# A hybrid SSD, short-convolution and PEER layer: the dt product placed among the first convolution tiles, and x and B made token-major by VectorE block transposes

## The reference, cut to what matters

```
h      = modulate(rmsnorm(x), shift, scale)        # 512 latent tokens; the same for 256 context tokens
z, xbc, dt, ... = split(h @ w_in)                  # xbc: 2048 columns (x 1024, B 512, C 512), dt: 32 columns
xbc    = silu(dwconv5(xbc) + bias)                 # 5 taps along the tokens
dt     = softplus(dt + dt_bias);  a = -exp(a_log) * dt
acs    = cumsum(a) within chunks of 128 tokens     # then exp(acs), exp(total), exp(total - acs)
states = B^T @ (exp(total - acs) * dt * x)         # per chunk; forward and backward, then a scan over chunks
mod_l  = silu(c) @ w_ada + b_ada                   # six rows of 1024; four of them are needed late
```

## Time and profile before

| what | value |
|---|---|
| plain executions | 1876.95 us median of 3 (1876.34 to 1878.25) |
| profiled execution | 1875.16 us, of which the span is 1873.4 us and 1.8 us lie around it |
| PE busy | 1432.9 us (76%), 4441 products |
| DVE busy | 1457.8 us (78%), 2813 instructions |
| ACT busy | 546.8 us (29%) |
| POOL busy | 870.1 us (46%) |
| busy tenths of PE, first ten of 40 slices (46.8 us each) | 7 9 9 9 9 9 9 8 8 8 |
| the same of DVE | 1 5 5 6 3 6 9 7 7 3 |

### The profile page before, as it was taken

One profiled execution on the slowest core, in us unless ns is written; L12 is line 12 of the kernel. 1 busy time (PEld: TensorE's weight loads), 2 busy tenths in 40 slices (PEclk: granted clock), 3 DMA queues, 4 the chain that ended last, 5 costly groups with the idle time before them and its releaser, 6 DMA issues.

```text
span 1873.4 us, 15554 instructions
## 1 busy us (share of the span) xinstructions
PE 1432.9 (76%) x4441; PEld 824.9 (44%) x4441; DVE 1457.8 (78%) x2813; ACT 546.8 (29%) x1558; POOL 870.1 (46%) x626
## 2 busy tenths in 40 slices
PE   7999999999888788787788677667655556565554
PEld 2565687888555555554555234334311111111111
DVE  1556369773887779888868888799989889898877
ACT  3100234522432343223312432233322223222222
POOL 0788510100455454443444465456655555555551
PEclk9999999999898999999998789889877776767776
DMA  9443312253999999999999999999999999999996
GB/s 380 192 152 142 139 62 84 91 200 111 411 386 421 421 421 421 421 422 421 421 421 421 399 398 421 421 423 421 421 421 422 421 422 422 421 422 421 422 422 250
DMA packets 91227, 652.50 MB, mean 348 GB/s; under 512 B 10494, under 2 KB 10886, under 8 KB 12806
## 3 DMA queue, kind: packets, MB, share of 16 engines
q0 software_dynamic: 76448, 555.78, 71.9%
q1 hardware_dynamic: 13808, 93.39, 12.6%
q10 hardware_dynamic: 887, 2.35, 0.3%
HBM read 649.37 MB, written 2.11 MB: 348 GB/s over the span
## 4 chain that ended last, share of the span: by engine, by line
DMA 42%; PE 27%; DVE 19%; issue 6%; ACT 4%; POOL 2%; SPq 0%; DVEq 0%; ACTq 0%; POOLq 0%
DMA arena<-in_peer_uv,arena 41%; PE bank L835 12%; DVE arena L2044 7%; PE bank L1128 5%; DVE arena L2080 4%; PE bank L1016 3%; POOL arena L767 2%; DMA arena<-in_w_ada 2%; PE bank L860 1%; PE bank L941 1%; PE bank L967 1%; ACT arena L1468 1%; DVE arena L2007 1%; PE bank L953 1%; DVE arena L1742 1%
## 5 line engine op out<-in xcount | busy, mean ns | idle before, releaser
L767 POOL DMA_INDIRECT arena<-in_peer_uv,arena x512 | 712.9, 1392 | 714.8 <-DVE arena L2080 430.9
L1128 PE MATMUL bank<-arena,smalls 128*128 128x512 f32 x1036 | 664.5, 777 | 411.0 <-ACT smalls L1476 405.5
L2044 DVE CUSTOM_DVE_ANT_0 arena<-arena 128x1024 f32<-128x1024 f32 x512 | 619.5, 1223 | 151.7 <-DMA arena<-in_peer_uv,arena 150.4
L1128 PEld LDWEIGHTS bank<-arena,smalls 128*128 128x128 f32 x1036 | 219.8, 230 | 776.6 <-ACT smalls L1476 575.2
L2080 DVE SCALAR_TENSOR_TENSOR arena<-arena 128x1024 f32<-128x1024 f32 x247 | 315.9, 1279 | 37.6 <-ACT arena L1468 34.4
L835 PE MATMUL bank<-arena 128*128 128x256 f32 (+1 forms) x1216 | 330.7, 430 | 2.2 <-ACT arena L1193 1.5
L1463 ACT ACTIVATE arena<-arena 128x2 f32<-128x2 f32 x255 | 51.9, 203 | 923.3 <-DVE arena L2044 923.2
L835 PEld LDWEIGHTS bank<-arena 128*128 128x128 f32 x1216 | 233.6, 193 | 102.4 <-issue 76.8
L1468 ACT ACTIVATE arena<-arena 128x1 f32<-128x1 f32 x510 | 122.5, 287 | 8.5
L1071 PE MATMUL bank<-arena 128*128 128x256 f32 x480 | 109.0, 380 | 0.0
L1476 ACT ACTIVATE smalls<-ident,arena 128x128 f32<-128x128 f32 x259 | 103.6, 401 | 8.3
(11 more groups left out here) (277 smaller groups left out, 1274.5 us busy)
## 6 DMA issues: line engine op xcount, KB each, us to landing
arena<-in_w_in SPq DMA_DIRECT2D x40, 1024.0 KB
arena<-in_w_ada POOLq DMA_DIRECT2D x16, 1024.0 KB, 5.1
arena<-in_w_out SPq DMA_DIRECT2D x16, 1024.0 KB, 12.9
arena<-in_peer_w_q SPq DMA_DIRECT2D x16, 1024.0 KB
arena<-in_w_ada SPq DMA_DIRECT2D x8, 1024.0 KB
arena<-in_peer_uv,arena POOLq DMA_INDIRECT x512, 23.9
arena<-in_x SPq DMA_DIRECT2D x4, 512.0 KB, 12.1
arena<-in_x_t SPq DMA_DIRECT2D x1, 2048.0 KB, 16.8
```

The source lines that it names most:

```text
L767: nc.gpsimd.indirect_dma_start(gslot[slot], None, uv_tab[0], bass.IndirectOffsetOnAxis(eid[t % 2][:, k:k + 1], 0)).then_inc(s_gsl[slot], 16)
L1128: last = mm(acc[h][:, :], diag[:, k % NDG], row_v(n)[:, h * 512:(h + 1) * 512], start=first, stop=last_one)
L2044: V.tensor_tensor_reduce(row_u(n), row_u(n), h2[t], 1.0, 0.0, ALU.mult, ALU.add, dots[:, k:k + 1]).then_inc(s_dot, 1)
```

## The change

The dt product moves behind the first channel tile (ct 0), the turn of dt behind ct 2, the decay products behind ct 8. DVE's and ACT's parts of that chain move into their convolution loops: DVE after ct 3, 4, 5, 10 and 12, ACT after ct 0, 3, 4 and 10. The latent x and B are no longer turned by PE and copied out: DVE turns them in SBUF with 16 block transposes for each pair of channel tiles (`turn_blocks`), after ct 3, 5, ... 13 and behind the `ada_piece` there. The context's x and B still go through PE (24 transposes), behind ct 13, and ACT copies them out after its silu of ct 14. The three z tiles after ada2 stand as before, with the transpose of the late rows ahead of the last. ACT's z gates now wait for all eight `ada_piece`s.

```diff
+        plan += {0: ["dtl", "dtc"], 2: ["dt"], 8: ["acs"],
+                 13: [(name, m, h) for m in range(LT, NT) for name, h in (("xsT", 0), ("xsT", 1), ("bT", 0))]}.get(ct, [])
+    plan += [("z", 0, 0), "ada2", ("z", 1, 0), ("z", 2, 0), "m2T", ("z", 3, 0)]
...
+            def context_turned():
+                pe.wait_ge(s_xb, 2 * NCTX)
...
+            BESIDE = {0: dt_product, 2: dt_turned, 8: decay_products, 13: context_turned}
...
+                if ct == 14:
+                    for m in range(LT, NT):
+                        for name, h, dst in (("xsT", 0, xs[:, m, 0:512]), ("xsT", 1, xs[:, m, 512:1024]), ("bT", 0, Bt[:, m])):
+                            ps = await_bank(act, (name, m, h))
+                            release(A(dst, ps[:, :], ACT.Copy), (name, m, h))
...
+            act.wait_ge(s_ared, NXB // 2)
+            for hq in range(3):
+                z_gate(hq)
...
+            def turn_blocks(pair):
+
+                dve.wait_ge(s_xb, 4 * pair + 4)
+                ct = 2 * pair
+                dst, col = (xs, ct * P) if ct < NX else (Bt, (ct - NX) * P)
+                for a in range(NBLK):
+                    for b in range(NBLK):
+                        i = xbl[32 * a:32 * a + 32, ct:ct + 2].rearrange("p k (m t) -> p k m t", t=P)
+                        o = dst[32 * b:32 * b + 32, 0:LT, col:col + 2 * P].rearrange("p m (k c) -> p k m c", c=P)
+                        V.transpose(o[:, :, :, 32 * a:32 * a + 32], i[:, :, :, 32 * b:32 * b + 32]).then_inc(s_xtr, 1)
...
                 if ct % 2 and ct > 1:
                     ada_piece(ct // 2 - 1)
+                if ct == 5:
+                    dve.wait_ge(s_dtl, 2)
+                    link(V.reciprocal(dte, dtu))
+                    link(V.tensor_tensor(dts[:], dts[:], dte, ALU.mult))
+                    link(V.tensor_tensor(dts[:], dts[:], dtl, ALU.add))
+                    link(V.tensor_tensor(dts[:], dts[:], dtx, ALU.add))
+                    link(V.tensor_scalar(alog[:], alog[:], -1.0, None, ALU.mult))
+                    link(V.tensor_tensor(adec[:], dts[:], alog[:].rearrange("p (d h) -> p d h", d=2).unsqueeze(2)
+                                         .to_broadcast(SM), ALU.mult))
+                    V.sem_inc(s_a, 1)
...
+                if ct % 2 and 1 < ct < NCTX + 2:
+                    turn_blocks(ct // 2 - 1)
```

More of the change, by code:

```diff
@@ L836, in project_T, with dt_product, dt_turned, decay_products @@
                 filled(last, name)
+            def dt_product():
+                pe.wait_ge(s_wdt, 16)
+                for name, h, n in (("dtl", lambda k: hTl[:, :, k, :], SEQ), ("dtc", lambda k: hTc[:, k, :], CTX)):
+                    dst = claim(name)[0:2 * HEADS, 0:n]
+                    if name == "dtl":
+                        dst = dst.rearrange("p (h n) -> p h n", h=2)
+                    for k in range(KD):
+                        last = mm(dst, wdt[:, k, :], h(k), start=(k == 0), stop=(k == KD - 1))
+                    filled(last, name)
+            def dt_turned():
+                ps = claim("dt")
+                await_read(pe, "dtl")
+                await_read(pe, "dtc")
+                for m in range(NT):
+                    last = tr(ps[:, m * 2 * HEADS:(m + 1) * 2 * HEADS], dtT[0:2 * HEADS, m * P:(m + 1) * P],
+                              ident[0:2 * HEADS, 0:2 * HEADS])
+                filled(last, "dt")
+            def decay_products():
+                pe.wait_ge(s_a, 1)
+                pe.wait_ge(s_const, 4)
+                ps = claim("acs")
+                NSC = NT * HEADS
+                ad = adec[:].rearrange("p d m h -> p (d m h)")
+                mm(ps[:, 0:NSC], upper[:], ad[:, 0:NSC], start=True, stop=True)
+                mm(ps[:, NSC:2 * NSC], lower[:], ad[:, NSC:2 * NSC], start=True, stop=True)
+                filled(mm(ps[:, 2 * NSC:4 * NSC], ones[:], ad, start=True, stop=True), "acs")
+            def context_turned():
+                pe.wait_ge(s_xb, 2 * NCTX)
+                for m in range(LT, NT):
+                    for name, h, ct in (("xsT", 0, 0), ("xsT", 1, 4), ("bT", 0, NX)):
+                        ps = claim((name, m, h))
+                        for k in range(4):
+                            last = tr(ps[:, k * P:(k + 1) * P], xbc_c[:, ct + k, (m - LT) * P:(m - LT + 1) * P], ident[:])
+                        filled(last, (name, m, h))
+            BESIDE = {0: dt_product, 2: dt_turned, 8: decay_products, 13: context_turned}
             for n in range(XBC // WCOL):
@@ L844, in _ @@
                         project_T(("xc", ct), w, j, lambda k: hTc[:, k, :])
[L846 to L853, removed]
+                    if ct in BESIDE:
+                        BESIDE[ct]()
             def z_part(hq, half, i):
@@ L868, in _ @@
                 if hq == 0:
[L869 to L875, removed]
                     ps = claim("ada2")
@@ L879, in _ @@
                     filled(mm(ps[:, 0:P], fold, apart, start=True, stop=True), "ada2")
+                if hq == 2:
+                    pe.wait_ge(s_mod2, 1)
+                    filled(tr(claim("m2T")[0:4 * KD, 0:P], mod2[:], ident[:]), "m2T")
             pe.wait_ge(s_xb, NXB + NCTX)
[L883 to L908, removed]
+            await_read(pe, ("bT", NT - 1, 0))
+            pe.wait_ge(s_xtr, N_XTR)
             def proj(n, half=0):
@@ L1218, in _ @@
                         ("z", hq, 0))
[L1220 to L1228, removed]
-            A(wst[:], wst[:], ACT.Exp).then_inc(s_edec, 1)
+            act.wait_ge(s_ared, NXB // 2)
+            for hq in range(3):
+                z_gate(hq)
             ps = await_bank(act, "m2T")
@@ new lines, in _ @@
+                if ct == 4:
+                    dve.wait_ge(s_dte, 1)
+                    link(V.tensor_scalar(dtu, dte, 1.0, None, ALU.add))
+                    V.sem_inc(s_dtx, 1)
+                    post(V.tensor_scalar(dts[:], dtu, -1.0, None, ALU.add))
+                    post(V.tensor_scalar(dtx, dtx, 0.0, None, ALU.max))
+                    settle()
+                    link(V.tensor_tensor(dts[:], dte, dts[:], ALU.subtract))
+                if ct == 5:
[8 more added lines that the diff above has]
+                    V.sem_inc(s_a, 1)
```

98 lines of the change are left out of this document (45 added, 53 removed).

## The result

| | before | after |
|---|---|---|
| executions, median of 4 each | 1877.28 us (1876.34 to 1878.25) | 1890.15 us (1888.02 to 1892.81) |
| ratio, 95% interval | | 1.0072 (1.006 to 1.0085) |
| profiled execution; its span | 1875.16; 1873.4 us | 1891.11; 1889.4 us |
| PE busy, products | 1432.9 us, 4441 | 1438.1 us, 4393 |
| DVE busy, instructions | 1457.8 us, 2813 | 1508.8 us, 2903 |

The changed kernel is slower by 0.6% to 0.85%, 12.9 us between the medians.

The account below looks back on a forecast made before the run. PE was taken to bound the kernel up to the first state product. 5.3 us saved, against later folds, DVE's lateness, a bank wait and half clock, put that product 12.8 us later: 1889.7 us, range 1875.5 to 1896.

Parts of the forecast that it names:

- What comes off, and what is moved: PE before the state product: 48 transposes go, 5.3 us off; the moved dt product delays folds 11.6 us, ada2 4.7.
- The block transposes: DVE behind odd channel tiles: 0.46 us each, 7.4 us for sixteen, as every one changes its partitions.
- The turns with POOL: Channel tiles: a DVE product with two SBUF operands waits until POOL's running one, up to 3.6 us, is over.
- rival 2: DVE's chain behind ct 3 and ct 5: scalar operations wait for POOL too, 2.5 us more, 1892.2 us; chance 0.18.
- ct 3's 4.1 us of chain: DVE behind ct 3: two short products, then one waiting for POOL's 3.6 us product, end at 4.1 us.
- POOL's own 0.3 us: Channel tiles, a sign to look for: POOL's own products 0.3 us longer beside DVE's softplus products.
- The bank wait: First z tile: its bank waits for ACT's context read behind ct 14's silu, so it starts at 230.0, not 213.3.
- The clock: PE's first z tile: half clock behind the idle time, losing 1.6 us.
- 1 (no lock): Channel tiles: DVE does not wait for POOL's long products; state product -0.6 to +1.0 us, 1876.3 to 1878.0; chance 0.25.
- 3: DVE's block transposes overlap, 5.5 us for sixteen, and the lock holds; ada2 waits, state product 255.5, 1881.5 us; chance 0.12.
- 4: DVE's block transposes take turns with POOL too or cost 11.2 us per sixteen: about 1909 us or more; chance 0.06.
- 5: State product: the whole 5.3 us comes, 1871.6 us, if ada2's chain through POOL does not move; chance 0.03.

Follow-up runs that it names:

- e6: Changed kernel with the dt product and its chain in the old place, context banks read behind ct 13, decay products before the last z tile: 1874.14 us, ratio 0.9989.
- e2: Changed kernel with the latent x and B turned by PE behind the z tiles again, so only the dt product and its chain moved: 1887.33 us, ratio 1.0054.
- e3: Changed kernel with DVE's 96 block transposes left out (stale x, constant B): 1877.09 us, one execution.
- e5: Changed kernel with each block transpose written to the 32 partitions it reads (wrong place for 12 of 16): 1882.68 us, one execution.
- e7: Changed kernel with ACT's six context copies behind its silu of ct 13, not ct 14: 1887.07 us, ratio 1.0052.
- e8: e7 with ada2 behind the third z tile and the late rows' transpose behind the fourth: 1888.82 us, ratio 1.0054.
- e4: Changed kernel with POOL's products of groups 2 and 3 left out (late modulation rows partly wrong): 1879.37 us, one execution.
- e1: Changed kernel with the dt product, its chain and the decay products in their old place, block transposes kept: 1878.32 us, ratio 1.0006.

## Why the prediction came out as it did

The forecast of 1889.7 us stands 0.5 from the median of 1890.15 (12.8 us forecast, 12.9 measured), and the state product, forecast at 263.7, came at 262.25. The path is the one forecast: folds late by the dt product, DVE late by the turns and the transposes, PE idle ahead of ct 14 and of z. By its steps:

**What comes off, and what is moved.** Right. 5.3 us off PE was worth 4.3 in e6, where one wait of 1.20 remains. The dt product alone moved the folds by 12.4 (e2) where the sum had 11.6, and the state product by 11.6; "ada2 late by 4.7 us even if DVE is never behind" was 5.09 (e3).

**The block transposes.** Forecast 0.46 us each, measured 0.466. Taking the price of those four rows that change partitions was right. The Trainium skill, "VectorE: DVE Perf Modes", section "Two Vector instructions with no wait between them", ties the hold to a change of the 32-partition group of input or output; e5, in which 12 of the output's 16 changes went and the input's order stayed, agrees: 0.36 against 0.466.

**The turns with POOL.** Right as a mechanism, too small in size behind ct 3. I had taken the scalar operations out of it. L1678, a scalar operation with one SBUF input, took 3.53 us with its wait and L1679 behind it 2.48: that is the mechanism of my rival 2, to which I gave 0.18. Its 1892.2 us did not come, because the 2.5 us shrank behind ct 3, as the table shows. In the Trainium skill, "SBUF — State Buffer", section "SBUF: two separate sides", the lock also holds for instructions in a two-port mode, and the trace agrees for this one in that it waited (no row says which mode it ran in); between L1683 and L1686 at 125.39 to 126.24 us in the changed kernel nothing waited, since POOL had no product then. In e3, where POOL had one, the scalar operation at 118.18 took 2.27 us.

The lateness of DVE at its tiles, from the start of a tile less the moment at which PE has it (ct 3 at 100.09, 10.32 for each tile, 0.77 for the decay products):

| tile | forecast, us late | start | measured |
|---|---|---|---|
| ct 4 | 7.2 | 120.06 | 9.7 |
| ct 5 | 3.8 | 126.64 | 5.9 |
| ct 6 | 16.4 | 148.98 | 17.9 |
| ct 7 | 11.5 | 154.30 | 12.9 |
| ct 8 | 14.6 | 167.68 | 16.0 |
| ct 9 | 9.7 | 173.00 | 10.2 |
| ct 10 | 12.8 | 186.37 | 13.3 |
| ct 11 | 10.4 | 194.67 | 11.3 |

The mis-sized term is ct 3's 4.1 us of chain, which was 6.5 (106.03 to 112.58). The error of 2.5 shrank along the row: ct 4 had 1.2 us of work where I had taken 1.5, ct 5's chain of 9.5 was 8.9 (132.59 to 141.50), and ct 9 gave 0.8 more back, since PE's decay products came ahead of it. Fold 4 ended at 200.7 (forecast 199.7), the last fold at 236.6 ("near 235.8"; the prediction's own terms, 218.3, 16.5 and 0.7, add up to 235.5, which moves no other term).

**POOL's own 0.3 us.** It did not come: in the channel tiles POOL's products keep their 3.59, 2.35 and 1.27 us, and only DVE waits. It moved no term, since the ledger used POOL's undisturbed lengths. But the reading of the earlier trace rows as a wait on either side stands, and the changed kernel shows the same pair again, DVE first, then POOL:

```profile
283.46 1.22 DVE L1746 TENSOR_TENSOR arena<-arena,smalls 128x1024 f32<-128x1024 f32 x1
283.63 1.52 POOL L703 TENSOR_TENSOR arena<-arena 128x256 f32<-128x256 f32 x1 [19.55 <-DVE arena L1785]
```

POOL's product, 0.61 us at its shortest, began 0.17 us behind DVE's and took 1.52, while DVE's kept the 1.22 us that it takes elsewhere. In the rows of ct 3 and ct 5 it is POOL that begins 0.07 to 1.2 us ahead of DVE, and DVE that waits. In all these rows the product that began second is the one that waited; the forecast did not ask which that would be.

**The bank wait.** z was forecast at 230.0 and started at 230.73. It was the wait that ended last, but e7 and e8 show that it was worth 0.8 to 2.0 us, because PE's lateness from ct 14 stands right behind it.

**The clock.** Half clock was placed at z (1.6 us), and came at ct 14, behind 8.55 us of idle time; z had only 2.79 ahead of it and ran in 7.17. So that term of the sum was 0 on the path, and with z 0.7 us late and some 0.5 less behind it the state product came 1.4 us early. The forecast named the idle time ahead of ct 14 among its signs, but its sum priced the clock at z alone, and nothing in it allowed for the 1.9 us behind 308.8. These two errors nearly cancelled: that the time came within 0.5 us is in part luck.

**The rivals.** 1 (no lock) falls by e4. 3 would have needed transposes at 5.5 us; e5, with 5.76, shows what it would have been: state product at 254.69, forecast 255.5 (with the 1.6 of PE's earlier start, 256.3). PE waited there ahead of ct 14 (4.83 us) and z (1.95), not ahead of ada2 as the rival had it. 4 falls by the 7.45 us beside a busy and an idle POOL. 5 falls by the folds, which came at 199.99 and 235.84 in place of 177.01 and 212.81, and by e1: even without the dt product's move nothing of the 5.3 comes as long as ACT reads behind ct 14.

**What stays open.** Why the clock fell behind 1.83 us of idle time in the changed kernel and in e3 to e6 and e8, and not in the kernel before, e1, e2 and e7, where the same instructions surround it; and why behind the 1.52 us ahead of ct 0 it fell in all but e3, e5 and e6. No run tests it. Each program has one trace, so the 1.9 us of the changed kernel is not shown to be a property of the change.

## What to carry to other kernels

Room on an engine in many small waits is spent once: the chain without the transposes left fold 4 at 187.8 us (1.0 of it the earlier start) and the transposes beside a quiet POOL at 190.0, both together at 200.0. When a product is moved ahead of a loop, follow each fold or release behind it to the engine that waits for it (here POOL, 36 us from fold 4 to the last), before counting what it frees at its old place. A chain of short dependent VectorE instructions beside long GpSimd products pays one GpSimd product per link, so put it where GpSimd is idle or behind the work that others wait for.

## What the runs showed of the hardware that I had not expected

- DVE and POOL wait for each other's products in SBUF, and in the rows shown it is the one that began second that waits: a 128x192 DVE product took 2.63 and 2.39 us in place of 0.36 behind POOL's, which stayed at 3.59 and 2.35; a 128x256 POOL product took 1.52 us in place of 0.61 behind DVE's, which stayed at 1.22. The wait stands inside the duration in the profile, not as idle time.
- A 128x192 fp32 scalar operation within SBUF waits in the same way (3.53 us against 0.26), a 32x256 block transpose doesn't (0.466 us beside busy and idle POOL alike).
- Block transposes of 32x256 come 0.466 us apart when each writes another group of 32 partitions than the one before, and 0.36 us apart when 12 of 16 write the same one (e5).
- PE's granted clock fell to 0.50 behind idle times of 8.55 us (the changed kernel, 212 to 216 us), 8.28 (e7), 7.71 (e2, 226 to 231 us), 5.09 (e3), 4.83 (e5) and 2.88 (e1, 207 to 210 us), but stayed at 1.00 behind 2.96 (e4) and 2.79 (the changed kernel), where the z tile took 7.17 us. Behind shorter ones it went either way: behind the 2.19 us ahead of the tile at 192.4 that tile took 7.13 us in the changed kernel and 8.83 in e7 (13.9 us for two at full clock), behind 1.95 us (e5) the z tile took 8.86, and behind 1.83 and 1.52 us the clock stayed at 1.00 in some programs and fell to 0.50 in others. So the length of the idle time alone does not order these cases.
